# Five of 31 convolution taps formed on GpSimd, and the token mixer's step loop written out

## The reference, cut to what matters

```python
def conformer_conv(a, g, hist, w_dw, b_dw, ln_g, ln_b):
    u = a * jax.nn.sigmoid(g)
    up = jnp.concatenate([hist, u], 1)
    y = lax.conv_general_dilated(up, w_dw[:, None, :], window_strides=(1,), padding='VALID',
                                 dimension_numbers=('NWC', 'WIO', 'NWC'),
                                 feature_group_count=CONV_CH) + b_dw
    y = jax.nn.silu(layer_norm(y, ln_g, ln_b))
    return y, up[:, -(CONV_K - 1):]
...
    h = x * (1 + sc1) + sh1
    proj = h @ w_in
    ...
    mix = jnp.concatenate([attn, conv], -1) @ w_out
    x = layer_norm(ALPHA * x + (1 + g1) * mix, ln1_g, ln1_b)
    h2 = x * (1 + sc2) + sh2
```

## Time and profile before

| what | us |
|---|---|
| median of 3 runs | 1634.87 (1630.88 to 1638.59) |
| the profiled execution | 1635.94 |
| its span, first to last instruction | 1634.2 |
| PE busy in the span | 1382.1 (85%) |
| DVE busy | 1302.3 (80%) |
| ACT busy | 798.1 (49%) |
| POOL busy | 531.9 (33%) |

### The profile page before, as it was taken

The page is one execution under the profiler, slowest core; times in us unless marked ns, Lnnn a source line. Parts: engine busy times, 40 slices in busy tenths (PEclk is TensorE's granted clock), DMA queues, the critical chain, the costliest instruction groups (busy, mean ns, idle before and its releaser), DMA issues. The chain is left out here.

```text
span 1634.2 us, 25729 instructions
## 1 busy us (share of the span) xinstructions
PE 1382.1 (85%) x7082; PEld 753.3 (46%) x7082; DVE 1302.3 (80%) x3336; ACT 798.1 (49%) x1443; POOL 531.9 (33%) x388
## 2 busy tenths in 40 slices
PE   5986899999999999999996653799999999997565
PEld 1113455565556656565554432344454444543121
DVE  0431999999999899989999217799999999995588
ACT  0411234444444334443444200689888988885122
POOL 0002115555544343555544340222222222220663
PEclk9997999999999999999998665799999999999798
DMA  9964102111101111111011018567997333222897
GB/s 310 398 231 148 36 1 78 53 53 52 52 29 42 46 39 52 52 52 52 39 43 41 26 59 289 181 227 240 342 340 281 104 114 116 103 103 103 238 332 246
DMA packets 90721, 218.28 MB, mean 134 GB/s; under 512 B 8035, under 2 KB 42759, under 8 KB 88592
## 3 DMA queue, kind: packets, MB, share of 16 engines
q1 hardware_dynamic: 65554, 136.25, 23.4%
q0 software_dynamic: 11808, 43.00, 8.9%
q10 hardware_dynamic: 13277, 38.20, 6.1%
HBM read 165.90 MB, written 51.56 MB: 133 GB/s over the span
## 5 line engine op out<-in xcount | busy, mean ns | idle before, releaser
L969 DVE SCALAR_TENSOR_TENSOR y_sum<-uT,w_dw_cols,y_sum 128x128 f32<-128x128 f32 (+1 forms) x1972 | 511.7, 348 | 0.0
L1687 DVE SCALAR_TENSOR_TENSOR w_gate_up_lo<-w_gate_up_ring,w_gate_up_hi 128x2048 f16<-128x2048 f16 x96 | 219.5, 2288 | 37.5 <-ACT w_gate_up_hi L1609 37.0
L1609 ACT ACTIVATE w_gate_up_hi<-w_gate_up_ring 128x2048 f16 x96 | 183.0, 1908 | 59.0 <-SPq L1567 39.5
L1096 PE MATMUL bank<-w_in_hi,hT_hi 128*128 128x512 f16 (+3 forms) x544 | 197.8, 364 | 12.8 <-ACT v L803 11.0
L1096 PE MATMUL bank<-w_in_lo,hT_hi 128*128 128x512 f16 (+3 forms) x544 | 197.1, 362 | 0.0
L1096 PE MATMUL bank<-w_in_hi,hT_lo 128*128 128x512 f16 (+3 forms) x544 | 196.9, 362 | 0.0
L1590 POOL COPY slot_index<-slot_token 128x1 int32 (+1 forms) x48 | 56.2, 1171 | 350.0 <-PE eturn L1751 307.3
L1730 PE MATMUL ps_up<-w_gate_up_hi,slot_rowsT_hi 128*128 128x512 f16 x384 | 147.0, 383 | 23.4 <-DVE slot_rowsT_lo L1712 18.1
L1730 PE MATMUL ps_up<-w_gate_up_lo,slot_rowsT_hi 128*128 128x512 f16 x384 | 146.6, 382 | 0.0
L1730 PE MATMUL ps_up<-w_gate_up_hi,slot_rowsT_lo 128*128 128x512 f16 x384 | 146.4, 381 | 0.0
L727 POOL TENSOR_TENSOR y_small<-y_small,mhalf 128x1 f32<-128x1 f32 (+1 forms) x17 | 9.4, 551 | 365.2 <-DVE y_small L1000 365.2
(11 more groups left out here) (256 smaller groups left out, 2884.8 us busy)
## 6 DMA issues: line engine op xcount, KB each, us to landing
w_ada_ring<-in_w_ada SPq DMA_DIRECT2D x12, 2048.0 KB, 14.0
expert_rows<-out_rows ACTq DMA_DIRECT2D x48, 512.0 KB
w_gate_up_ring<-in_w_gate SPq DMA_DIRECT2D x16, 1024.0 KB
w_gate_up_ring<-in_w_up SPq DMA_DIRECT2D x16, 1024.0 KB
w_down_ring<-in_w_down SPq DMA_DIRECT2D x16, 1024.0 KB
x_h<-in_x_prompt SPq DMA_DIRECT2D x16, 512.0 KB
x_res<-in_x_prompt SPq DMA_DIRECT2D x16, 512.0 KB, 3.3
hidden<-h SPq DMA_DIRECT2D x16, 512.0 KB, 2.6
```

What stands on the lines that cost most here:

```text
L969: dve.scalar_tensor_tensor(total, u, w, y_sum[:, c, :n], ALU.mult, ALU.add).then_inc(taps_done, 1)
L1096: mm = pe.matmul(out, x[xp][:, k, :n], w[wp][:, k, cols], start=(k == 0 and wp == xp), stop=(k == KD - 1 and xp == 1))
L1609: act.activation(gate_up_parts[0][:, at, k:k + KD // 2, :, :].rearrange("p k a n -> p (k a n)"), w_gate_up[:, bass.ds(b, 1), k:k + KD // 2 ...
L1687: dve.scalar_tensor_tensor(flat[1], w_gate_up[:, bass.ds(b, 1), k, :, :].rearrange("p b k a n -> p (b k a n)"), W_SCALE, flat[0], ALU.mult ...
```

## The change

For tiles 1 to 14 GpSimd forms taps 26 to 30. Per channel block it multiplies `uT` with the first tap's weight into `u_out` (the buffer that is otherwise idle), and then four times multiplies into a scratch tile `tap` and adds `tap` to `u_out`. That is 5 multiplications and 4 additions a block, 36 instructions a tile, and each instruction of a block but the first waits by semaphore for the one before it. VectorE does taps 0 to 25 into `y_sum`, and then one addition per block, `y = y_sum + u_out`. Its portions are cut anew by `FEWER_CUTS`. GpSimd does its block as the first thing in the step, ahead of `y_small`; it starts when `uT` of the tile is there and all tap sums of the tile before it are done (`u_out` has one buffer). Apart from this, all engines' steps of the mixer are now written out instead of looped.

```diff
+        tap = sb("tap", [P, P])
...
         TAP_CUTS = (10, 12, 13, 15, 22, 26, 28)
+        FEWER_CUTS = (8, 10, 11, 13, 19, 22, 24)
+        POOL_TAPS = 5
+        FEWER = TAPS - POOL_TAPS
+
+        def shared_taps(j):
+
+            return isinstance(j[0], int) and 1 <= j[1] <= TILES - 3
+
+        def shared_before(j):
+            return min(max(j[1] - 1, 0), TILES - 3)
...
+                def taps(j):
+                    p, n = j[1] % 2, rows_of(j)
+                    pool.wait_ge(uT_ready, count(1, j, 1))
+                    if j[1] >= 2:
+                        pool.wait_ge(carried, count(3, j, -3))
+                    if j[1] == 1:
+                        pool.wait_ge(cache_stored["sample"], 16 * 4)
+                    else:
+                        pool.wait_ge(taps_done, count(TAP_OPS, j))
+                    for c in range(CB):
+                        done = (shared_before(j) * CB + c) * POOL_TAPS
+                        total = u_out[:, c * P:c * P + n]
+                        for x in range(POOL_TAPS):
+                            k = FEWER + x
+                            u = M["uT"][:, p, c, k:k + n]
+                            w = M["w_dw"][:, c, k:k + 1]
+                            if x == 0:
+                                pool.tensor_scalar(total, u, w, None, ALU.mult).then_inc(pool_taps, 1)
+                            else:
+                                pool.wait_ge(pool_taps, done + x)
+                                pool.tensor_scalar(tap[:, :n], u, w, None, ALU.mult).then_inc(tap_ready, 1)
+                                pool.wait_ge(tap_ready, (shared_before(j) * CB + c) * (POOL_TAPS - 1) + x)
+                                pool.tensor_tensor(total, tap[:, :n], total, ALU.add).then_inc(pool_taps, 1)
+
                 def step(i):
+                    if (j := lagged(i, 1)) is not None and shared_taps(j):
+                        taps(j)
                     if (j := lagged(i, 2)) is not None:
                         n = rows_of(j)
...
-                    for k in range(first, last):
+                    for k in range(first, min(last, FEWER) if shared_taps(j) else last):
...
+                    if shared_taps(j) and last == TAPS:
+                        for c in range(CB):
+                            dve.wait_ge(pool_taps, (shared_before(j) * CB + c + 1) * POOL_TAPS)
+                            dve.wait_ge(taps_done, count(TAP_OPS, j, (FEWER - 1) * CB + c + 1))
+                            dve.tensor_tensor(y[:, p, c, :n], y_sum[:, c, :n], u_out[:, c * P:c * P + n], ALU.add).then_inc(taps_done, POOL_TAPS)
...
-                over_steps(dve, step, first=-1)
+                for i in range(-1, TILES + 3):
+                    step((0, i))
```

More of the change, by code:

```diff
@@ L598, in mix @@
         taps_done = sem("taps_done")
+        tap_ready = sem("tap_ready")
+        pool_taps = sem("pool_taps")
         y_stats = sem("y_stats")
@@ L701, in step @@
                             sp.dma_start(v_out[0:WIN - SMP], M["vprev"][SMP:WIN, 0, :]).then_inc(stored, 16)
-                over_steps(sp, step)
+                for i in range(TILES + 3):
+                    step((0, i))
                 sp.wait_ge(h2_stored, 16 * TILES)
@@ L776, in _ @@
                 modulate((0, 0))
-                over_steps(pool, step)
+                for i in range(TILES + 3):
+                    step((0, i))
             @block.scalar
@@ L940, in step @@
                         act.copy(mixT[0][:, 0:4, :n], turn_bank("o", 0)[:, :, :n]).then_inc(oT_hi_ready, 1)
-                over_steps(act, step, first=-1)
+                for i in range(-1, TILES + 3):
+                    step((0, i))
             @block.vector
@@ L989, in step @@
                     if j1 is not None:
-                        taps(j1, 0, TAP_CUTS[0])
+                        cuts = FEWER_CUTS if shared_taps(j1) else TAP_CUTS
+                        taps(j1, 0, cuts[0])
                     if j2 is not None:
@@ L1014, in step @@
                     if j1 is not None:
-                        taps(j1, TAP_CUTS[0], TAP_CUTS[1])
+                        taps(j1, cuts[0], cuts[1])
                     if j3 is not None:
@@ L1027, in step @@
                     if j1 is not None:
-                        taps(j1, TAP_CUTS[1], TAP_CUTS[2])
+                        taps(j1, cuts[1], cuts[2])
                     if j3 is not None:
@@ L1038, in step @@
                     if j1 is not None:
-                        taps(j1, TAP_CUTS[2], TAP_CUTS[3])
+                        taps(j1, cuts[2], cuts[3])
                     if j1 is not None:
@@ L1044, in step @@
                     if j1 is not None:
-                        taps(j1, TAP_CUTS[3], TAP_CUTS[4])
+                        taps(j1, cuts[3], cuts[4])
                     if j1 is not None:
@@ L1052, in step @@
                     if j1 is not None:
-                        taps(j1, TAP_CUTS[4], TAP_CUTS[5])
+                        taps(j1, cuts[4], cuts[5])
                     if j0 is not None:
@@ L1066, in step @@
                     if j1 is not None:
-                        taps(j1, TAP_CUTS[5], TAP_CUTS[6])
+                        taps(j1, cuts[5], cuts[6])
                     if j1 is not None:
-                        taps(j1, TAP_CUTS[6], TAPS)
+                        taps(j1, cuts[6], TAPS)
                     if (j := lagged(i, -1)) is not None:
@@ L1227, in step @@
                         turn_in(i, "o", 0, [(c, o_tok[:n, c * P:(c + 1) * P], n, P) for c in range(4)], o_turned)
-                over_steps(pe, step, first=-1)
+                for i in range(-1, TILES + 3):
+                    step((0, i))
 def load_expert(sp, a, W, e, b):
```

## The result

The changed kernel takes 1727.7 us (median of 4 runs, 1723.9 to 1728.4). Beside it stand 4 runs of the kernel before, 1630.9 to 1647.1; the ratio is 1.0544 (95% interval 1.0488 to 1.06): 5.4% slower. The profiled execution is 1727.8 us, 91.9 above the one before.

The account below looks back on a forecast made before the run. PE and VectorE looked nearly full, but the ring T1 + T2 + T3 was taken to set the step: 600.2 + 10.2 - 590.0 = +20.4 on 1635.9 gives 1656.3, so 1655 beside the median; range 1617 to 1690.

Parts of the forecast that it names:

- the price of the multiplication: GpSimd's multiplication of a 128-column tile by a weight per partition, taken as 340 ns, 20 of them a tile.
- T2: From the end of uT on ACT to GpSimd's start of y_small; 13.8 us without a loop return, forecast 16.4.
- much slower: Rival: multiplication costs the addition's 455 ns, T2 18.7, all 13 steps followed by slow stretches; +62 us, 1697; chance 0.16.
- The ring: Chain of waits in the mixer closing once a step, T1 + T2 + T3; forecast 13 x (14.8 + 16.4 + 14.97) = 600.2 us.
- T1: From PE's turn of h2 to the end of uT on ACT; taken as 14.8 us.
- T3: From GpSimd's y_small to PE's turn of h2; taken as 14.97 us where PE waits.
- Tile 1's block: GpSimd's first block of taps, left out of the 13 steps counted because no h2 lies behind it.
- The slow stretches: Stretches behind PE's longer waits for h2 with PE at 1.2 GHz, 1.7 us each; 6 of 13 counted, 10.2 us.
- VectorE's relief: 20 taps less 4 additions a tile off VectorE, 60 us of busy time over 14 tiles, counted at nothing.
- the five returns: The loop's returns to its top, removed by writing it out: 5 x 2.7 plus 5 x 1.7 us, 22 us gained.
- The first signs: Expected in the changed profile, including VectorE's 2.6 us pieces gone, block starting at uT's end, PE waiting 2 us for h2.
- the signs of being wrong: Block beginning later than uT, GpSimd gaps above 0.07 us, PE waiting for something else, or PE stretches waiting for nothing.

Follow-up runs that it names:

- the list of single instructions: Kernel before, with single GpSimd instructions added in the idle setup, each waiting for the one before it; 1638.6 us in one run.
- the cheaper form: Changed kernel, five taps on GpSimd, each multiplication written as a product of two tiles with the weight's column repeated; 1661.0 us, ratio 1.0149.
- Relief alone: Changed kernel without GpSimd's taps and VectorE's four additions; taps 26 to 30 of tiles 1 to 14 left out; 1607.3 us, ratio 0.9797.

## Why the prediction was wrong, point by point

It said 1655, within 1617 to 1690, slower with 0.56. The sign was right and so was the mechanism; the size was far out.

- **The step that failed: the price of the multiplication.** I took 340 ns, "a third of the way from the affine select to the addition", with the addition's 455 as the upper bound. It is 605. Twenty of them are 20 x 0.265 = 5.3 us of the 5.9 by which T2 was missed (22.26 for 16.4); the gaps, 0.09 instead of 0.07, are the rest: 32 x 0.02 = 0.6. The bound was no bound: it ordered instructions by how many tiles they read, and nothing in the rows had shown that order. The rival "much slower" named the scalar per partition as an extra read. By the list of single instructions that is 80 ns of the 265; the rest is the form, which costs 528 by a constant too. And it stopped at the same 455.
- **The ring was right.** With the measured T2 its own formula gives 13 x (14.8 + 22.26 + 14.97) - 590.0 = +86, 1722 us; measured 1728. T1 stayed, and T3 lost 0.3. The four kernels with other blocks lie on the same line: steps of 46.74 at a T2 of 17.28, 47.08 at 17.65, 51.7 at 22.26, and 43.77 where T2 is below 13.9 and T3 undisturbed.
- **Tile 1's block, counted at nothing, cost 8 us.** It "has no `h2` behind it", but it has `y_small` of tile 0 behind it, and PE's turn of that tile's `y_tok`. GpSimd's `y_small` of tile 0, before and with the change:

```profile
204.76 0.55 POOL L727 TENSOR_TENSOR y_small<-y_small,mhalf 64x1 f32<-64x1 f32 x1 [35.25 <-DVE y_small L1000]
```

```profile
214.46 0.57 POOL L767 TENSOR_TENSOR y_small<-y_small,mhalf 64x1 f32<-64x1 f32 x1
```

  It is 9.7 us late, of which 1.7 were there ahead of the block (`uT` of tile 1 ends at 192.21, before at 190.51).
- **The slow stretches, counted at +10 us, cost some 2.** They are there, in every step: behind PE's wait for `y_tok` the granted clock is 0.50, 1.2 GHz, and then 1.00 again.

```profile
418.00:421.00 3.00, 2.94 (x14) 2.32 (x15) 2.79 (x13) 2.25 (x7) 2.86 (x3) 0.50 0.00 0
421.00:430.00 9.00, 8.73 (x53) 4.86 (x51) 8.82 (x34) 6.83 (x22) 5.29 (x4) 1.00 0.16 59
```

  Before, PE waited for `h2` and the slow stretch fell into T1, on the ring. Now it falls between `y_tok` and `h2`, where PE must wait for `h2` anyway, still by 0.29 us at 430.02; only in two of the twelve steps did it reach past that (T3 of 15.6 and 15.5). The kernels with four taps and with the cheaper form, where PE waits some 0.8 and 1.1 us a step for `y_tok` and 1.7 for `h2`, show no slow stretch in these steps at all.
- **VectorE's relief at nothing, the five returns at 22 us, VectorE's taps not slowed by the block:** right for the steps. Relief alone leaves the step at 43.77, written-out code gains 21.7 us by H(12) and its steps show no price for fetching it, three hidden taps cost nothing, and VectorE's taps take 0.26 us beside the block.
- **The first signs named for it** came: the pieces of 2.6 us ahead of VectorE's first tap gone, the block beginning at the end of `uT`, `y_small` released by GpSimd's own work, VectorE idle ahead of its `y_small`. PE's wait stands at `y_tok`, not at `h2`, where I had put it: the earlier of the two turns takes the delay. Of the signs of being wrong two came: gaps above 0.07, and PE waiting for something else than `h2`.

Together: 13 x 5.86 = +76 for T2, -8 for the slow stretches, +8 for tile 1 and some -4 for a T3 of 14.64 in place of 14.97 are the 72 us between 1656.3 and the profiled 1727.8. That the stretches and tile 1 cancel is chance.

The Trainium skill, GPSIMD Engine Reference, section 4.1 (Engine selection), which has one-input work on GpSimd near line rate, would have led further off still. Row and rule differ for the multiplication: 1562 ns for 512 columns with one tile as input, 1260 with two. For the copy, 609, they do not. The rows that the prediction set beside the page's first half bear it out less than it says: 1269 ns for 512 columns is 1.2 times VectorE's 4 x 0.27 us, and the 455 ns worked out for 128 columns are 1.7 times its 0.27.

## What to carry to other kernels

Find the ring that closes once a step, and give an idle engine only work that fits into the slack of its piece: three taps in 12.3 us were free, the fourth, 4.9 us more, cost 45. An instruction that the trace does not show has no upper bound from rows of other kinds: here it cost twice the nearest row and a third more than the bound; if the sum hangs on it, it is measured by itself first. Before an edit is counted as a gain, ask what the freed engine was last to end: here the useful half of the change was the loop, and the half that moved the work was worth nothing as the kernel stood, whatever its price.

## What was not expected of the hardware

- GpSimd's `TENSOR_SCALAR` with a weight per partition takes 608 ns for 128 columns and 1562 for 512, more than a `TENSOR_TENSOR` addition (452, 1260), and the same product by a repeated column takes 400 and 1048.
- VectorE's one-column instruction with two inputs in SBUF waits behind GpSimd's instructions with two tiles as input: it takes 0.16 us when it starts first, up to 1.21 behind one `v`, and 4.88 behind four where GpSimd came out of 13.8 us of work without a stall. The Trainium skill, SBUF — State Buffer, section Who interferes with whom, has the two contend in this case; that it can last over several of GpSimd's instructions is what the trace adds.
- GpSimd's 0.09 to 0.10 us between dependent instructions vanish when two chains alternate: the same 36 instructions last 13.8 us instead of 17.6.
